# Low halves of a mixer's weights on one engine and in place, the order of that engine's program, and another order of work in front of the experts

## What is computed

```python
h  = x @ w_in                                  # 2048 -> 5120, ten chunks of 512 columns
y_a = b_gate * causal_dwconv(c_gate * xa, conv_a)        # 3 taps, 1024 channels
y_b = u * (block-causal w_s @ layer_norm(v) + bias)      # 512 channels
y_c = silu(layer_norm(causal_dwconv(ca * sigmoid(cg), conv_c) + b))  # 31 taps, 512
x1 = layer_norm(alpha * x + concat(y_a, y_b, y_c) @ w_out)   # four chunks of 512
# router: sigmoid(x1 @ w_router), 8 groups of 4 experts, best group, top 2 in it
# experts: (silu(x1 @ w1[e]) * (x1 @ w3[e])) @ w2[e], 32 experts of 2048 -> 512 -> 2048
out = layer_norm(alpha * x1 + gated sum of the experts)
```

## Time and profile before

| | us |
|---|---|
| median of 3 runs | 1376.84 (1372.6 to 1377.66) |
| the profiled execution | 1375.04 |
| its span, first to last instruction | 1372.9 |
| granted TensorE clock, mean share of full | 0.972 |
| PE busy | 1268.6 (92%) |
| VectorE, ACT, POOL busy | 414.4, 319.6, 244.2 |
| transfers | 472.30 MB, mean 344 GB/s |

### The profile page before, as it was taken

The page is one execution under the profiler, slowest core; times in us unless marked ns, Lnnn a source line. Parts: engine busy times, 40 slices in busy tenths (PEclk is TensorE's granted clock), DMA queues, the critical chain, the costliest instruction groups (busy, mean ns, idle before and its releaser), DMA issues.

```text
span 1372.9 us, 15741 instructions
## 1 busy us (share of the span) xinstructions
PE 1268.6 (92%) x6914; PEld 725.9 (53%) x6914; DVE 414.4 (30%) x574; ACT 319.6 (23%) x529; POOL 244.2 (18%) x62
## 2 busy tenths in 40 slices
PE   3897998999999999999999999999999999999993
PEld 2896998988864444444444444344444434444331
DVE  5635999372233120120211202011120211202026
ACT  4332332443342221112211122111112111121101
POOL 2757767656600000000000000000000000000001
PEclk7998999999989999999999999999999999999997
DMA  8463554546767999999999999999999999999991
GB/s 294 147 215 123 161 178 135 173 153 215 277 257 298 418 431 428 427 427 427 427 427 427 427 429 428 427 427 427 428 427 428 428 427 429 427 427 428 427 390 66
DMA packets 62921, 472.30 MB, mean 344 GB/s; under 512 B 7058, under 2 KB 7634, under 8 KB 37250
## 3 DMA queue, kind: packets, MB, share of 16 engines
q1 hardware_dynamic: 59568, 469.83, 83.6%
q10 hardware_dynamic: 3282, 1.43, 0.5%
HBM read 469.14 MB, written 2.10 MB: 343 GB/s over the span
## 4 chain that ended last, share of the span: by engine, by line
PE 69%; DMA 16%; DVE 10%; ACT 2%; POOL 1%; issue 1%; SPq 0%; ACTq 0%; DVEq 0%
PE psum L679 30%; PE psum L723 9%; PE psum L481 9%; DMA area_g<-in_w_dram 8%; PE psum L503 7%; PE psum L619 7%; DMA ring<-in_w_dram 6%; DVE area_g L1114 5%; PE psum L642 3%; PE psum L643 2%; POOL w_low L419 1%; ACT area_c L942 1%; DVE area_a L1192 1%; PE psum L596 1%; DVE w_low L1093 1%
## 5 line engine op out<-in xcount | busy, mean ns | idle before, releaser
L679 PE MATMUL psum<-ring,area_c 128*64 128x512 f32 x1536 | 348.3, 599 | 6.5 <-DMA ring<-in_w_dram 6.5
L419 POOL TENSOR_TENSOR w_low<-ring,w_high 128x2048 fp32r<-128x2048 f32 (+1 forms) x42 | 225.1, 5367 | 114.5 <-ACT w_high L804 114.5
L679 PEld LDWEIGHTS psum<-ring,area_c 128*64 128x64 f32 x1536 | 105.0, 137 | 207.7 <-issue 204.8
L481 PE MATMUL psum<-in_high,w_high 128*128 128x256 f32 x576 | 167.7, 291 | 24.7 <-POOL w_low L419 9.3
L942 ACT ACTIVATE area_c<-psum,gain 128x128 f32<-128x128 f32 x256 | 96.2, 456 | 359.2 <-PE psum L619 359.2
L427 POOL TENSOR_TENSOR area_b<-area_b,slot 128x1024 f32<-128x1024 f32 x1 | 3.2, 3227 | 983.6 <-ACT area_b L1004 983.6
L1379 DVE TENSOR_TENSOR area_a<-area_a,psum 128x512 f32<-128x512 f32 x64 | 43.9, 686 | 419.6 <-PE psum L643 402.3
L723 PE MATMUL psum<-ring,area_d 128*64 128x512 f32 x768 | 167.9, 593 | 0.8 <-ACT area_d L978 0.5
L481 PE MATMUL psum<-in_low,w_high 128*128 128x256 f32 x576 | 166.4, 289 | 0.0
L481 PE MATMUL psum<-in_high,w_low 128*128 128x256 f32 x576 | 166.2, 289 | 0.0
L804 ACT ACTIVATE w_high<-ring 128x2048 fp32r<-128x2048 f32 x56 | 107.0, 1914 | 185.6 <-PE psum L481 114.3
(11 more groups left out here) (174 smaller groups left out, 1127.1 us busy)
## 6 DMA issues: line engine op xcount, KB each, us to landing
ring<-in_w_dram SPq DMA_DIRECT2D x142, 2048.0 KB, 24.2
slot<-in_w_dram SPq DMA_DIRECT2D x24, 2048.0 KB, 21.5
area_g<-in_w_dram SPq DMA_DIRECT2D x24, 2048.0 KB, 26.0
ring<-in_w_in_dram SPq DMA_DIRECT2D x40, 1024.0 KB, 5.0
ring<-in_w_out_dram SPq DMA_DIRECT2D x16, 1024.0 KB, 5.1
ring<-in_w_dram SPq DMA_DIRECT2D x4, 1024.0 KB, 21.3
area_a<-in_x_dram SPq DMA_DIRECT2D x2, 1024.0 KB, 7.7
out_dram<-area_b SPq DMA_DIRECT2D x4, 512.0 KB, 2.6
```

Of the source, the lines that this page charges most:

```text
L419: nc.gpsimd.tensor_tensor(low[:, tiles], raw_unit(u)[:, tiles], high[:, tiles].bitcast(F32), ALU.subtract).then_inc(pool_low, 1)
L481: mm = pe.matmul(o[:, c, :], w[a][:, k, c * P:(c + 1) * P], in_part[b][:, kk, :], start=kk == 0 and a + b == 0 and c % 2 == 0, stop=kk == ...
L679: mm = pe.matmul(psum[i * CAP:(i + 1) * CAP, j // UNITS, :], gathered[:, kk, i * CAP:(i + 1) * CAP], w[i][:, r, :], start=kk == 0, stop=kk ...
```

## The change

All low halves of the weights are made by VectorE, each written over its raw unit (`w_low[q]` lies where raw buffer q lies), so a raw buffer is free when PE has used the unit. The three high halves and `in_low` move down, the last slot of the ring is free during the mixer, and becomes expert slot 2. VectorE's program is written out by units: `low(u)` for every unit, and between two of them about two taps or another piece. The mean and variance matmuls of y_c go behind units 0 and 2 of channels(8). The last unit of an output chunk takes tile 0's products first, and `residual` treats the tiles one after the other. Logits of chunks 0 to 2 are gathered in one bank in four row groups, brought to SBUF and folded by a matmul with `fold`; chunk 3's are added (`logits_rest`). No `spread_rows` stands in front of the ranks, all four are in step 0, behind j = 3 to 6. ACT normalises groups 0 and 1, VectorE groups 2 and 3. In each step the gate matmul and gathers 2 and 3 stand behind j = 1, and the transposes go to banks 0 and 1 without waiting for the next step's gathers to be drained.

```diff
-        w_part = [[nc.alloc_sbuf_tensor_at(f"w_{name}{b}", [P, UNIT, CW], F32R,
-                                           offset=ring_at + raw_bytes + 4 * U_LEN * (2 * b + i))
-                   for i, name in enumerate(("high", "low"))] for b in range(SPLITS)]
+        w_high = [nc.alloc_sbuf_tensor_at(f"w_high{b}", [P, UNIT, CW], F32R, offset=ring_at + raw_bytes + 4 * U_LEN * b)
+                  for b in range(SPLITS)]
+        w_low = [nc.alloc_sbuf_tensor_at(f"w_low{q}", [P, UNIT, CW], F32R, offset=ring_at + 4 * U_LEN * q)
+                 for q in range(UNITS)]
...
-        slots = [slot0[:], flat_g] + [ring[:, i, :] for i in range(SLOTS - 2)]
+        slots = [slot0[:], flat_g, ring[:, SLOTS - 3, :]] + [ring[:, i, :] for i in range(SLOTS - 3)]
...
@@ -286,13 +292,7 @@
                 else:
                     src = w_out[0][:, (n - N_IN) * CW:(n - N_IN + 1) * CW]
                 if u >= UNITS:
-
-                    if u == UNITS:
-                        sp.wait_ge(first_low, 1)
-                    if q < UNITS - 1:
-                        sp.wait_ge(pool_low, pool_lows(u - UNITS + 1))
-                    else:
-                        sp.wait_ge(dve_low, n)
+                    sp.wait_ge(units_done, u - UNITS + 1)
...
-            sp.wait_ge(pool_low, pool_lows(N_UNITS - 2))
             load_expert_unit(2, 2, 0)
-            sp.wait_ge(pool_low, pool_lows(N_UNITS))
-            sp.wait_ge(dve_low, N_MIX)
+            sp.wait_ge(units_done, N_UNITS - 2)
             load_expert_unit(3, 3, 0)
             sp.wait_ge(units_done, N_UNITS)
...
-            for u in range(N_UNITS):
-                if u == 1:
-                    for k in range(1, GROUPS):
-                        input_low(k)
-                if u % UNITS < UNITS - 1:
-                    pool.wait_ge(high_ready, u + 1)
-                    high, low = w_part[u % SPLITS]
-                    tiles = slice(0, UNIT // 2 if u == 0 else UNIT)
-                    nc.gpsimd.tensor_tensor(low[:, tiles], raw_unit(u)[:, tiles], high[:, tiles].bitcast(F32),
-                                            ALU.subtract).then_inc(pool_low, 1)
+            for k in range(1, GROUPS):
+                input_low(k)
...
+                pe.wait_ge(low_ready, u + 1)
+                return w_high[u % SPLITS], w_low[u % UNITS]
...
-                        pe.wait_ge(in_high, TT * KT // 4 + q + 1)
-                        pe.wait_ge(in_low, GROUPS + q + 1)
-                    for k in range(UNIT):
+                        pe.wait_ge(in_high, TT * KT // 4 + (1 if q == 0 else UNITS))
+                        pe.wait_ge(in_low, GROUPS + (1 if q == 0 else UNITS))
+                    by_tile = n >= N_IN and q == UNITS - 1
+                    order = [(k, t) for k in range(UNIT) for t in range(TT)]
+                    if by_tile:
+                        order.sort(key=lambda at: at[1])
+                    for k, t in order:
                         kk = UNIT * q + k
-                        for t in range(TT):
-                            for a, b in PRODUCTS:
-                                mm = pe.matmul(o[:, t, :], in_part[a][:, kk, t * P:(t + 1) * P], w[b][:, k, :],
-                                               start=kk == 0 and a + b == 0, stop=kk == KT - 1 and a == 1)
+                        for a, b in PRODUCTS:
+                            mm = pe.matmul(o[:, t, :], in_part[a][:, kk, t * P:(t + 1) * P], w[b][:, k, :],
+                                           start=kk == 0 and a + b == 0, stop=kk == KT - 1 and a == 1)
+                        if by_tile and (k, t) == (UNIT - 1, 0):
+                            mm.then_inc(tile0_done, 1)
                     mm.then_inc(units_done, 1)
...
-            pe.wait_ge(z_used, 1)
-            pe.wait_ge(conv_c_step, TAPS_C * CT)
...
+            def mean_c():
+
+                pe.wait_ge(z_used, 1)
+                pe.wait_ge(conv_c_step, TAPS_C * CT)
...
+            def variance_c():
+
+                pe.wait_ge(c_sq, 1)
...
+            channels(8, {0: mean_c, 2: variance_c})
...
                         mm = pe.transpose(psum[:, 6 + t, j * P:(j + 1) * P], area_a[:, t, at:at + P], ident[:])
                     mm.then_inc(r_turned, 1)
 
-            def logits(c):
...
+            def logits_part(c):
 
                 if c == 0:
                     pe.wait_ge(drained[2], 4)
+                pe.wait_ge(r_kept, TT * (c + 1))
+                for j in range(CT):
+                    mm = pe.matmul(psum[j * E:(j + 1) * E, 4, 0:SEQ], w_scaled[:, CT * c + j, :],
+                                   area_d[:, CT * c + j, :], start=c == 0, stop=c == NC - 2, skip_group_check=True)
+                if c == NC - 2:
+                    mm.then_inc(part_ready, 1)
+
+            def fold_part():
+
+                pe.wait_ge(part_kept, 1)
                 for t in range(TT):
-                    pe.wait_ge(r_kept, TT * c + t + 1)
-                    for j in range(CT):
-                        k = CT * c + j
-                        mm = pe.matmul(psum[:, 4, t * E:(t + 1) * E], area_d[:, k, t * P:(t + 1) * P],
-                                       w_scaled[:, k, :], start=k == 0 and t == 0, stop=k == KT - 1,
-                                       skip_group_check=True)
-                return mm
+                    pe.matmul(psum[:, 5, t * E:(t + 1) * E], logit_part[:, t * P:(t + 1) * P], fold[:],
+                              start=t == 0, stop=False, skip_group_check=True)
+
+            def logits_rest():
+
+                for t in range(TT):
+                    pe.wait_ge(r_kept, TT * (NC - 1) + t + 1)
+                    for k in range(KT - CT, KT):
+                        mm = pe.matmul(psum[:, 5, t * E:(t + 1) * E], area_d[:, k, t * P:(t + 1) * P],
+                                       w_scaled[:, k, :], start=False, stop=k == KT - 1, skip_group_check=True)
+                mm.then_inc(logits_ready, 1)
 
...
 
             tokens(N_IN)
             tokens(N_IN + 1, {1: [(turn_sums, 0)]})
-            tokens(N_IN + 2, {1: [(turn_sums, 1)], 2: [(logits, 0)]})
-            tokens(N_IN + 3, {0: [(logits, 1)], 1: [(turn_sums, 2)], 2: [(logits, 2)]})
+            tokens(N_IN + 2, {1: [(turn_sums, 1)], 2: [(logits_part, 0)]})
+            tokens(N_IN + 3, {0: [(logits_part, 1)], 1: [(turn_sums, 2)], 2: [(logits_part, 2)]})
             turn_sums(3)
-            logits(3).then_inc(logits_ready, 1)
-            spread_rows(0)
-            spread_rows(1)
+            logits_rest()
 
...
-                    if j < 2:
-                        if j == 0:
-                            if behind:
-                                pe.wait_ge(gt_drained, it)
-                            slot_gates(it, s)
-                        else:
-                            pe.wait_ge(slot_gates_kept, it + 1)
+                    if j == 1:
+                        if behind:
+                            pe.wait_ge(gt_drained, it)
+                        slot_gates(it, s)
                         if first:
-                            pe.wait_ge(normed, 2 * TT + TT * (3 + j))
-                        gather(it, s, 2 + j)
+                            pe.wait_ge(normed_late, 2 * TT)
+                        gather(it, s, 2)
+                        pe.wait_ge(slot_gates_kept, it + 1)
+                        gather(it, s, 3)
                     if behind and 2 <= j < 2 + NC:
                         combine(it - 1, j - 2)
-                    if first and j in (3, 5):
-                        spread_rows((j + 1) // 2)
+                    if first and 3 <= j < 3 + NC:
+                        spread_rows(j - 3)
                 if ahead:
                     pe.wait_ge(onehot_ready, it + 2)
                     gather(it + 1, 1 - s, 0)
                     gather(it + 1, 1 - s, 1)
                 pe.wait_ge(hidden_ready, it + 1)
-                if ahead:
-                    pe.wait_ge(gather_drained, 4 * it + 5)
                 for f in range(FT):
-                    mm = pe.transpose(psum[:, 2, f * P:(f + 1) * P], hidden[:, f * P:(f + 1) * P], ident[:])
+                    mm = pe.transpose(psum[:, 0, f * P:(f + 1) * P], hidden[:, f * P:(f + 1) * P], ident[:])
                 mm.then_inc(ht_ready, 1)
-                if ahead:
-                    pe.wait_ge(gather_drained, 4 * it + 6)
                 for t in range(TT):
-                    mm = pe.transpose(psum[:, 3, t * P:(t + 1) * P], one_hot[:, s, t, :], ident[:])
+                    mm = pe.transpose(psum[:, 1, t * P:(t + 1) * P], one_hot[:, s, t, :], ident[:])
                 mm.then_inc(gt_ready, 1)
                 pe.wait_ge(ht_drained, it + 1)
                 if behind:
...
+            for g in range(UNITS // 2):
...
-                    keep_gathered(it + 1, (0, 1))
+                    keep_gathered(it + 1, (0,))
                 act.wait_ge(ht_ready, it + 1)
```

(62 more changed lines are left out.)

227 lines of the change are left out of this document (133 added, 94 removed).

## The result

The changed kernel takes 1336.25 us, the median of 4 runs (1335.35 to 1336.87). The kernel before took 1375.96 beside it (1372.6 to 1377.66). The ratio is 0.9713, with a 95% interval of 0.97 to 0.9726: 39.7 us faster. The profiled execution took 1336.75, with a span of 1335.0.

A forecast was written before the change was run, and what follows sets the result against it. The weight transfers bound the end, from the moment their stream is continuous (request at 424.5). Span 1372.9 - 28.3 - 0.5 - 4.7 + 3.8 = 1343.2, execution adds 2.1: 1345.3; forecast 1346 us, range 1340 to 1358.

The forecast's parts named there:

- (4): Router: first expert unit 15.9 us after the mixer's end instead of 20.6, bounds 14.5 and 18; gain 4.7.
- (3): Start: VectorE makes the first low half whole, alone; TensorE starts 0.5 us sooner, bounds 0 and 1.
- (5): Step 0 of the expert stage: later slot releases leave the stream dry behind four; 3.8 us lost, bounds 2.5 and 5.
- (6): Later expert steps: 0.8 us less of TensorE's step, hidden by the transfers, so 0; last step and final norm stay.
- (1): Mixer: with all low halves on VectorE, no TensorE waits left; bounds 0 and 8 us, removable part 28.3.
- (2): Mixer, low halves in place: raw units load later, with cover of 7.9 us in the ring; taken as 0.
- the logits, folded early, end before that chain does: Router, last mixer unit: the logits finish before VectorE's residual and statistics chain; no size given.
- a microsecond before 424.5 is worth one of the whole: Expert stage's start: time saved before the ninth half is requested counts fully; inside later steps nothing while TensorE's step is under 58.9.
- A: Rival, mixer: VectorE becomes the bound in part; two late pieces give 1358, chance 0.14; slow taps 1376, 0.04.
- C: Rival, mixer: raw loads tied to TensorE make it slower, 1432 if a load takes 19.7 us; chance 0.04.
- B: Rival, expert stage's start: last four of eight halves still arriving, so TensorE 2.5 us quicker brings nothing more; no separate chance.
- all gains at their better end: Lower end of the range: 33 us off, 1342, less some scatter of runs, giving 1340.

The follow-up runs named there:

- e3: The changed kernel with the router's logits taken as before the change (1.71 us of TensorE for each of chunks 0 to 2 instead of 0.57): 1339.20 us, ratio 0.9742.
- e2: The changed kernel, with GpSimd also doing 35 subtractions of low-half size on data that nothing uses: 1388.47 us, ratio 1.0102.
- e10: The changed kernel, but GpSimd makes three of four low halves again, except those of units 0 to 3, which VectorE makes: 1355.36 us, ratio 0.9842.
- e4: The changed kernel with the first low half shared between GpSimd and VectorE as before: 1337.97 us, ratio 0.9731.
- e8: The changed kernel with the spreading of the norm's rows left out (each spread matmul covers one column): 1333.86 us, ratio 0.97.
- e1: The changed kernel, but GpSimd makes three of four low halves again, new order and places kept: 1370.22 us, ratio 0.9964.

## Why the prediction was off

The mechanism was right and six sizes were off, all but one in the same direction. The step that failed is in part (4): the router's logits stand there only as work that ends early enough, and the change of what they cost TensorE in the mixer was put at nothing. It was 3.4 us, the largest of the six, and undoing it in e3 ends the mixer 3.0 later. Against the sum of 1343.2 the span is 1335.0, 8.2 less:

| term | predicted | measured | difference |
|---|---|---|---|
| start of TensorE (3) | -0.5 | -2.0 | -1.5 |
| logits of chunks 0 to 2, in no term | 0 | -3.4 | -3.4 |
| first chunk's own slow matmuls and the rest | -28.3 | -29.8 | -1.5 |
| mixer end to first expert unit (4) | -4.7 | -4.0 | +0.7 |
| step 0 gives back (5) | +3.8 | +2.8 | -1.0 |
| last landing to the end (6) | 0 | -1.4 | -1.4 |

That makes -8.1. Another 1.5 is on the way from span to median: I added 2.1 and 0.7, and the profiled execution lies 1.75 above its span and 0.5 above the median.

**(1) Low halves: right.** I forecast no wait, and there is none in 305 us. The taps gave back 30 us and not 43, because I had set two measures against each other: 0.37 is the busy time for each of 20 taps that overlap, 0.73 the mean duration of one. In busy time a tap took 0.65 (78.5 for 120) and takes 0.41 (48.8 for 120). Yet VectorE's share is 0.70, not 0.75, and a low half and eight taps (2.29 and 3.25) fit into a unit of 5.76, as forecast. That the taps and low halves pay for GpSimd is shown by e2, and that sharing makes the waits by e10.

**(2) In place: right.** The old order of loads cost nothing to give up; no wait for a raw unit or a high half is in the mixer.

**(3) Start: wrong size.** The bound of 0 to 1 came from the halved operation's length. GpSimd's half stood in VectorE's way as well: half the low half and `in_low` took 3.11 and 1.68 in the chain before, the whole and `in_low` take 2.20 and 0.61 now. The rows before:

```profile
26.50 3.11 DVE w_low L1078
29.61 1.68 DVE in_low L1062
```

Mutual exclusion, which I had read from the earlier trace rows for the taps, I didn't apply to the two operations in front of the first matmul. e4 gives the 2.2 back.

**(4) Router: the failed step is "the logits, folded early, end before that chain does".** That they end early is true; I asked only where they stand and not what they cost. The matmuls of chunks 0 to 2 were turned round, 8 where there were 16: 0.57 instead of 1.71, three times, is 3.4 us of the mixer's own time. The diff shows it in one line, and no term of the sum has it. The rest of the step came out: 16.6 for 15.9, the gather 6.73 and 6.18 in the two traces where I had taken 6.1, at granted clocks of 0.55 and 0.60. The Trainium skill (TensorE: Matmul & The Clock Gate, Part 1) has the throttled state as the default. By that the whole gather would have run slow, some 7.5; with 6.73 at 0.55 the trace lies between the two readings.

**(5) Step 0: releases right, what they are worth wrong.** Counted from the first expert unit they came at 7.1, 18.4, 29.3, 40.3 and 52.3, where I had 7.2, 18.7, 29.7, 40.7 and 52.7. What was wrong in (5) too is the sentence "a microsecond before 424.5 is worth one of the whole". The stream starts there, but it isn't continuous from there, not in the kernel before either. It is continuous from the fifth pair on, and everything in front of it counts only through it. That gives 52.3 - 49.5 = 2.8, simpler than my sum over four gaps, and it holds for every kernel here but e8, where it is at its limit. By my own release times it would have given 52.7 - 49.3 = 3.4. The 871.5 can be worked out too: 175 further halves at 4.91 and 8.3 us to the first landing make 867.6, and about 4 stay, for which there are the five late landings (see the tail, above).

The issue rows of the changed kernel, which that rests on:

```profile
427.89 0.33 SPq L312 DMA_DIRECT2D slot<-in_w_dram  x1
...
slot<-in_w_dram SPq DMA_DIRECT2D x1, 2048.0 KB, 8.3
```

**(6) Later steps: nothing, as forecast, up to the last landing.** TensorE's step fell by 1.3 instead of 0.8, and the waits for transfers took it up. What I had fixed as "the last step stays" did stay, counted from the landing that TensorE starts it with: 86.3 and 86.1. That the tail is 1.4 shorter comes, but for 0.2, from one late landing that fell behind this one and not in front of it. The sum has no term for that, and no row read before the change could have told it.

Rivals A and C needed a wait in the mixer, and there was none. B, the cap by the last four of eight halves, was all but reached: the eighth half landed at 382.4, 23.3 behind the mixer's end where I had 20.5, and the ninth was asked for at 382.7. It cost nothing, because the end hangs on the fifth pair.

The range failed at its lower end: I had set it at "all gains at their better end", where the gains were those that I had listed. A missed term of 3.4 us isn't covered by any bound on the listed ones.

## What to carry to other kernels

Find the moment from which the stream never runs dry again, and measure every edit by what it does to that moment; here it is the release of the fifth pair, not the first request. When two durations are compared, both must be busy time or both the duration of one operation. A helper engine that reads the same memory beside VectorE can cost more than it makes: 35 operations that nothing uses cost 52 us. And go through the diff for each matmul that changes its shape, also where it stands under other work: on the engine that sets the time its length counts wherever it stands.

## What was not expected of the hardware

- VectorE and GpSimd stood still until the other's operation was over, some 3.5 us of one of 3.78 in e2, where I had thought of both going slower side by side.
- After a wait of 2.7 us TensorE's first matmuls sometimes ran slow and sometimes not. Two steps of the changed kernel, each behind a wait of 2.7 for a transfer, in TensorE's order of time and in the chain (32 matmuls each):

```profile
1249.02 8.66 PE L693 MATMUL psum<-ring,area_c 128*64 128x512 f32 x32 [2.71 <-DMA ring<-in_w_dram]
```

```profile
953.88 7.09 PE psum L693 x32
```

The same work takes 8.66 in the one, at a mean granted clock of 0.81, and 7.09 in the other, at 1.00. What tells the two apart, no run here shows.
- The runs of e1 lie 12.7 us apart (1359.02 to 1371.74), those of the changed kernel 1.5 (1335.35 to 1336.87). Where the two engines contend, small shifts of order seem to decide between waits; that was not tested.
